# A gated branch sum in a hybrid decoder layer: the product kept in its PSUM bank instead of a buffer in SBUF

## The reference

```
z      = x @ w_in                       # inputs of the four mixers, and four gates of 1024 columns
y_a, y_b, y_c, y_d = four mixers of z   # RG-LRU, Conformer convolution, pooling, short convolution
merged = sigmoid(gate_0) * (y_a @ w_branch[0])
for n in 1, 2, 3:
    merged = merged + sigmoid(gate_n) * (y_n @ w_branch[n])
x = LN(alpha * x + merged @ w_out)
x = LN(alpha * x + SwiGLU(x))
```

## Time and profile before

| | |
|---|---|
| median of 3 runs | 958.42 us (957.92 to 959.2) |
| the profiled execution | 958.29 us, span 956.5 us |
| TensorE matmul busy | 931.3 us, 97% of the span |
| VectorE busy | 619.9 us, 65% |
| ScalarE busy | 382.8 us, 40% |
| GpSimd busy | 376.7 us, 39% |
| granted TensorE clock, mean | 0.997 of full speed |

### The profile page before, as it was taken

One profiled execution on the slowest core, in us unless ns is written; L12 is line 12 of the kernel. 1 busy time (PEld: TensorE's weight loads), 2 busy tenths in 40 slices (PEclk: granted clock), 3 DMA queues, 4 the chain that ended last, 5 costly groups with the idle time before them and its releaser, 6 DMA issues.

```text
span 956.5 us, 18924 instructions
## 1 busy us (share of the span) xinstructions
PE 931.3 (97%) x7382; PEld 926.5 (97%) x7382; DVE 619.9 (65%) x929; ACT 382.8 (40%) x597; POOL 376.7 (39%) x288
## 2 busy tenths in 40 slices
PE   6999999999999999999999999999999999999995
PEld 6999999999999999999999999999999999999995
DVE  2699999995203888443444699988888788411125
ACT  4323232325536323323232366555455557322223
POOL 4656565666363354354455353000000003434424
PEclk9999999999999999999999999999999999999998
DMA  8533333223222322322334221433433343432202
GB/s 240 158 89 98 88 97 88 77 77 88 67 67 68 99 84 82 99 86 79 99 88 142 68 64 26 133 88 93 125 89 88 103 116 91 146 91 83 77 1 94
DMA packets 166802, 89.35 MB, mean 93 GB/s; under 512 B 4650, under 2 KB 164690, under 8 KB 166753
## 3 DMA queue, kind: packets, MB, share of 16 engines
q1 hardware_dynamic: 164521, 87.75, 32.2%
q10 hardware_dynamic: 2232, 0.92, 0.3%
HBM read 85.49 MB, written 3.17 MB: 93 GB/s over the span
## 4 chain that ended last, share of the span: by engine, by line
PE 87%; DVE 9%; ACT 1%; POOL 1%; issue 1%; DMA 1%; SPq 0%; DVEq 0%; POOLq 0%
PE main L1093 56%; PE main L1326 19%; PE aux L1326 3%; PE main L1242 3%; PE aux L1093 2%; DVE aux L1562 1%; PE main L1443 1%; PE aux L1079 1%; POOL x_lo L623 1%; PE aux L1242 1%; DMA x_tok<-in_x_prompt 1%; DVE merged L1742 1%; DVE main L1739 0%; DVE aux L1774 0%; DVE scr L1646 0%
## 5 line engine op out<-in xcount | busy, mean ns | idle before, releaser
L537 POOL TENSOR_TENSOR w_lo<-raw,w_hi 128x1024 fp32r<-128x1024 f32 (+1 forms) x128 | 282.4, 2210 | 531.4 <-ACT w_hi L660 529.4
L1093 PE MATMUL main<-x_hi,w_lo 128*128 128x272 f32 x1024 | 212.3, 288 | 1.3 <-DVE x_lo L1465 1.2
L1093 PE MATMUL main<-x_hi,w_hi 128*128 128x272 f32 x1024 | 211.9, 288 | 0.0
L1093 PE MATMUL main<-x_lo,w_hi 128*128 128x272 f32 x1024 | 211.1, 288 | 0.0
L660 ACT ACTIVATE w_hi<-raw 128x1024 fp32r<-128x1024 f32 x128 | 135.0, 1058 | 145.5 <-PE main L1093 138.6
L1093 PEld LDWEIGHTS main<-x_hi,w_lo 128*128 128x128 f32 x1024 | 160.8, 188 | 1.8 <-DVE x_lo L1465 1.5
L1093 PEld LDWEIGHTS main<-x_lo,w_hi 128*128 128x128 f32 x1024 | 160.8, 188 | 0.0
L1093 PEld LDWEIGHTS main<-x_hi,w_hi 128*128 128x128 f32 x1024 | 159.9, 189 | 0.0
L1093 PE MATMUL main<-y,w_hi 128*128 128x272 f32 x512 | 84.6, 287 | 0.0
L1562 DVE SCALAR_TENSOR_TENSOR aux<-glu_pad,miscT,aux 128x512 f32<-128x512 f32 x112 | 75.1, 747 | 0.0
L767 ACT ACTIVATE sig<-main 128x544 f32<-128x544 f32 x32 | 20.0, 626 | 131.1 <-PE main L1093 131.1
(11 more groups left out here) (366 smaller groups left out, 2138.0 us busy)
## 6 DMA issues: line engine op xcount, KB each, us to landing
raw<-in_w_in SPq DMA_DIRECT2D x64, 512.0 KB, 4.1
raw<-in_w_ff_gate SPq DMA_DIRECT2D x22, 512.0 KB, 4.0
raw<-in_w_ff_up SPq DMA_DIRECT2D x22, 512.0 KB, 5.0
raw<-in_w_branch SPq DMA_DIRECT2D x32, 256.0 KB, 3.5
raw<-in_w_ff_down SPq DMA_DIRECT2D x16, 512.0 KB, 3.9
raw<-in_w_out SPq DMA_DIRECT2D x8, 512.0 KB, 3.9
raw<-in_w_ff_down SPq DMA_DIRECT2D x8, 384.0 KB, 3.3
x_tok<-in_x_prompt SPq DMA_DIRECT2D x4, 512.0 KB, 6.8
```

Of the source, the lines that this page charges most:

```text
L537: pool.tensor_tensor(w_lo[s][:, 0:n, :], raw[s][:, 0:n, :], w_hi[s][:, 0:n, :].bitcast(F32), ALU.subtract).then_inc(w_lo_ready, 1)
L1093: mm = pe.matmul(ps[:, h, :], w[s][:, k, :], x[:, h * HALF:(h + 1) * HALF], start=(first and k == 0 and j == 0), stop=(last and k == n - 1 ...
```

## The change

In rounds 1 to 3 the multiply writes its result back into `slot(1)`, the two PSUM banks that it reads. VectorE waits for it, then adds `slot(1)` to `merged`. The increment of `tile_out[1]`, which hands the banks back to TensorE, moves from the multiply to the add. VectorE's wait for the add stays in round 3 alone, ahead of the split. The buffer `prod` goes; its place in SBUF is given to nothing else.

```diff
-        prod = at("prod", [P, NT], F32, at_sm + 3 * CH + 128)
...
-                ve.tensor_tensor(halves(prod[:, :]), slot(1), halves(sig[mm][:, :]), ALU.mult)\
+                after(link(ve.tensor_tensor(slot(1), slot(1), halves(sig[mm][:, :]), ALU.mult)))
+                ve.tensor_tensor(halves(merged[:, m, :]), halves(merged[:, m, :]), slot(1), ALU.add)\
                   .then_inc(tile_out[1], 1)
-                ve.wait_ge(tile_out[1], i * 2 + ((U_MIX + 16 * q) // 2 + mm + 2))
-                v = link(ve.tensor_tensor(merged[:, m, :], merged[:, m, :], prod[:, :], ALU.add))
-                after(v)
                 if q == 3:
+                    ve.wait_ge(tile_out[1], i * 2 + ((U_MIX + 16 * q) // 2 + mm + 2))
                     split(merged[:, m, :], Y_C[:, m, :], Y_A[:, m, :]).then_inc(merged_ready, 1)
```

## The result

| | before | changed |
|---|---|---|
| median | 958.17 us (957.48 to 959.2, 6 runs) | 962.94 us (961.62 to 963.87, 6 runs) |
| ratio | | 1.0046, 95% interval 1.0035 to 1.0058 |
| profiled execution, span | 958.29 us, 956.5 us | 962.95 us, 961.2 us |
| granted clock, mean | 0.997 | 0.995 |

The change costs 4.8 us where the sum had 1.4.

The account below looks back on a forecast made before the run. TensorE, 97% busy, was taken as the bound, moved only by when VectorE hands slot(1) back. 0.88 + 0.88 - 0.35 = +1.4 us gave a median of 959.8 us, range 958.6 to 961.0.

Parts of the forecast that it names:

- The sign of the extra time: Whole kernel: the change was forecast to make it slower, by +1.4 us, to a median of 959.8 us.
- Within 0.2%: Whole kernel: a time that measurement cannot tell from no change, about 1.9 us; chance 0.76.
- the slower case: Whole kernel: a time slower by more than the 0.2% that measurement can tell; chance 0.21.
- B's: Rival: less is lost, through closer overlap or an output projection not held by the release; 958.8 us; chance 0.11.
- the term of -0.35: Round 1 behind the first stall: without the add wait VectorE no longer holds TensorE, giving back 0.35 us, 0.45 at most.
- Hand-over and its two places: Release after multiply, wait and add: 0.88 us later, paid at round 1's first product and the output projection's start.
- what is behind shifts plainly: Behind the output projection's start: later stretches keep their times and only shift, giving nothing back.
- The margins of 0.3 and 0.65 us: Round 1, second and third product: VectorE's release was to come this much before TensorE needs it.
- Rival A: Round 1: VectorE's recurrence runs into GpSimd's subtractions; 0.35 not given back, 0 to 1.5 us on top; 960.9 us; chance 0.20.
- Rival C, the clock: Longer TensorE gaps lower the granted clock from 2.4 to 1.2 GHz, costing 3 us more; 963 us; chance 0.03.
- Cover in round 2: Rounds 2 and 3: VectorE is early, and about 5 us of cover hides the later release at no cost.

Follow-up runs that it names:

- e6_small_subtractions: The changed kernel with GpSimd's low-part subtractions for round 1's weights cut to one of eight (or four) chunks; 961.57 us, ratio 1.0026.
- e4_no_add_wait: The kernel before, early release kept, without VectorE's wait for the add in rounds 1 and 2, with two product buffers in turn; 958.92 us, ratio 1.0005.
- e11_before_small: The kernel before with GpSimd's subtractions of round 1 cut to one of eight (or four) chunks; 958.12 us, ratio 0.9997.
- e5_filler: The changed kernel with 12 unread matmuls filling TensorE's idle time behind the second gate unit of round 1; 962.13 us, ratio 1.0038.
- e10_filler_and_small: The changed kernel with both 12 idle-filling matmuls in round 1 and GpSimd's round 1 subtractions cut to one of eight (or four) chunks; 959.84 us, ratio 1.0011.
- e2_rounds23_only: The kernel before with the change made in rounds 2 and 3 alone; 959.98 us, ratio 1.0015.
- e1_round1_only: The kernel before with the change made in round 1 alone; 962.35 us, ratio 1.0036.
- e3_late_in_sbuf: The changed kernel with the product written to the SBUF buffer prod again, the release still on the add; 963.36 us, ratio 1.0054.
- e7_first_product_early: The kernel before, without the add wait in rounds 1 and 2, and with round 1's first product ahead of the first decay; 963.44 us, ratio 1.006.
- e8_after_first_early: The changed kernel with the first product of round 1 ahead of the first decay; 964.08 us, ratio 1.0057.

## Why the prediction was wrong

**The sign of the extra time** was right (959.8, a sum of +1.4), the size was not: 962.94 lies outside 958.6 to 961.0. "Within 0.2%" had 0.76, and the slower case that came had 0.21. (The lower end was called B's, whose own price is 958.8; that changes nothing.) The sum was short by 3.2 us of the span. Two things make up 3.07 of them: 1.52 at the term of -0.35, and 1.55 at the clock, which the sum had at nothing.

**Hand-over and its two places: right.** Forecast 0.88 us each, measured 0.86 in round 1 and 0.89 at the output projection. The multiply was forecast at 733 ns (733), the add at 724 (722). The add from PSUM was no slower than the one of before (747). That speaks against what the Trainium skill's fixed cycles would make of it ("VectorE: DVE Perf Modes", section "The TRN2 errata — SBUF-src ops pay a fixed extra latency per instruction"). That what is behind shifts plainly was right to 0.1 us.

**The term "-0.35, TensorE runs at 9.00 us behind the first stall": the step that failed.** The seven last intervals came out 1.17 us longer, not 0.35 shorter; the eight that were to be 72.1 to 72.3 us are 75.27, low clock included. The margins of 0.3 and 0.65 us were computed with VectorE's durations of before, though the two engines had moved against each other. GpSimd follows TensorE, VectorE runs on its own, and what GpSimd's catches cost in a step went from 3.0 to 4.6 us. Rival A named this mechanism and was given 0.20; its point of decision, 0.65 us more in the second step, was passed with 3.2 us lost in the decay. `e6_small_subtractions` shows it: with most of GpSimd's work gone, the seven intervals are 9.00 to 9.02. The reason that I gave for the term was wrong as well. I had VectorE's time without its wait for the add close the small waits of round 1. `e4_no_add_wait` drops that wait alone and gains 0.1 us; `e11_before_small` keeps it and gains 0.45. Those small waits were GpSimd's. What was caught is of two kinds: instructions with two inputs in SBUF (L1647, L1648, L1650, L1657, L1666), and the copies and one-input instructions that take 0.17 and 0.44 us alone (L1646, L1662, L1665). The Trainium skill, "SBUF — State Buffer", section "Who interferes with whom", has a VectorE instruction with two SBUF inputs or in a two-port mode block against a GpSimd read for its whole length. The trace agrees for the first kind; the mode of the second it does not show. Multiply and add, which have one input in PSUM, kept 733 and 722 ns.

**Rival C, the clock: given 0.03, and it came.** I held an idle of 3.09 us at a clock of 1.00 against it. That idle lies near the start, where TensorE had hardly worked; the new one lies between two dense stretches. Whether that is what tells them apart no run shows. The price, 3 us, was twice the measured 1.55. `e5_filler` and `e10_filler_and_small` show that the idle is the cause; `e5_filler` shows that half of the gain is then paid as waits.

**A and C together were in no case.** I priced each alone. Both hang on one event, the later first release, and could come together.

**Cover in round 2: missed.** I took 15 waiting products for all of rounds 2 and 3. The first of round 2 did not wait for TensorE and had 0.5 us of cover; alone, that place costs 0.5 us (`e2_rounds23_only`). In the changed kernel, where TensorE comes late already, it takes 0.07 and, behind the restart, 0.11 us.

**Off the list:** that each product costs a little, and that PSUM costs by itself, fell with `e1_round1_only`, `e2_rounds23_only` and `e3_late_in_sbuf`.

Open: in which executions the clock falls after a stall of 2.1 us. It did in four of five profiles, and by the mean clock in 25 of 33 executions.

## What to carry to other kernels

Put the release of a bank on the first instruction that no longer needs it; a buffer in between that looks like waste buys the next engine its start, here 0.9 us at each place where it waits. Before calling a shift harmless, find the places where the margin is small by hand, product by product, and count again there which instructions run beside a slow one of another engine once the two have moved against each other. Take a stall between dense matmuls at more than its length when it grows past what the trace before has shown.

## What was not expected of the hardware

- An idle of 2.1 us of TensorE in the middle of dense work was followed by about 4 us with the clock partly at its lower level (0.58 and 0.57 in two stretches), in four of five profiles. Idles of 1.23 us at the same place and of 1.75 us ahead of the output projection were followed by no low stretch in any profile. After 5.5 us it was 7 us.
- A copy of eight columns (128x8) took 1.96 us instead of 0.17 beside a GpSimd subtraction, and a 128x544 instruction 2.93 instead of 0.71. A shift of 0.5 to 2 us between the two engines turned 3.0 lost microseconds of a step into 4.6.
- Two cures that gave 0.7 and 1.6 us alone gave 3.15 together (sums of the nine intervals: 86.73, 86.02, 85.13, and 83.58 with both): the low clock and the waits for GpSimd had covered one another.
- Inside a GpSimd subtraction an add with both inputs in SBUF took 1.83 us (`e7_first_product_early`), and one with an input in PSUM 0.72 us (`e8_after_first_early`).
